# The last attention groups of a second block: softmax moved a round ahead, copies of probabilities first, one projection in halves

## The chip, the cores and the metric

The kernel runs on one core of a Trainium2 chip as a single launch. The metric is the device time of that launch in microseconds (us). A core has five engines that run their own instruction streams in order: TensorE (PE in the rows; PEld is its weight load), VectorE (DVE), ScalarE (ACT), GpSimd (POOL) and SyncE (SP), which here only issues loads. They meet through semaphores: an instruction waits until a counter that another engine raises has reached a value.

## The reference, cut to what matters

The program runs two blocks one after the other, each two layers deep, on 256 tokens of width 1024 in fp32. The first block (attention, then a mixture in which each token gathers 128 expert rows) takes most of the time and isn't touched. The second block's layer has four kinds of attention side by side, then an output projection and a wide feed-forward part:

```python
for l in range(DEPTH):                                   # 2 layers
    h = rms_norm_2(x, norm1_g[l])
    proj = h @ w_in[l]
    (a_cq, a_ckv, a_kr, b_q, b_k, b_v, c_q, c_k, c_v, d_q, d_k, d_v) = jnp.split(proj, splits, axis=-1)
    y_a = mla_mixer(a_cq, a_ckv, a_kr, ...)              # 4 heads, keys and values from a latent
    y_b = diff_mixer(b_q, b_k, b_v, ...)                 # 4 heads, difference of two softmaxes, then a norm per head
    y_c = swa_mixer(c_q, c_k, c_v, swa_sinks[l], ...)    # 4 heads, window of 128, a sink in the softmax
    y_d = na_mixer(d_q, d_k, d_v, na_rpb[l])             # 4 heads, a table of biases
    mix = jnp.concatenate([rms_norm_2(y_a, out_g_mla[l]), y_b,
                           rms_norm_2(y_c, out_g_swa[l]), rms_norm_2(y_d, out_g_na[l])], axis=-1)
    x = x + mix @ w_out[l]
    h = rms_norm_2(x, norm2_g[l])
    x = x + jnp.square(jax.nn.relu(h @ w_up[l])) @ w_down[l]
return rms_norm_2(x, final_norm_g)
```

## The kernel before, in words

Every engine has its own function (`pe_program`, `act_program`, `dve_program`, `sp_program`, `pool_program`), written out by hand in the order in which that engine shall run; nothing reorders it later. What one engine needs of another is a `wait_ge(*at(name, ...))`.

The attention of a layer of the second block is cut into ten groups, in the order `ORDER = ("d0", "d1", "d2", "d3", "m0", "m1", "w0", "w1", "n0", "n1")`: d are the difference heads, m the latent ones, w the window, n the table of biases; the digit of m, w and n is the half of the tokens. A group passes through these steps:

- scores on TensorE (`scores`) into one of two pairs of banks of the accumulator PS, used in turn;
- bias and row maximum on VectorE (`bias_and_max`). For w and n the bias is added into a buffer in BIG first, which frees the pair of banks; for d and m the maximum is read from PS;
- exponentials with row sums on ScalarE (`softmax`);
- sums turned into reciprocals on VectorE (`row_sums`), for d also the difference of the two softmaxes;
- transposes of the probabilities on TensorE (`p_transposes`) into the four single banks of PS, copied back to BIG by `evac_pT`: the even bank by ScalarE, the odd one by VectorE;
- the product with the values on TensorE (`values`), into a single bank again, and its scaled copy into H by VectorE (`attended`).

All engines run a loop of twelve rounds r. In round r TensorE makes the scores of group r, the values of group r-3 and the transposes of group r-2, and between them some other product: the projections C0, C1, D0, D1, D2 of the normed tokens (`project`), the lift of the latents (`lift`, rounds 0), and towards the end the transposes of finished sections (`mixed_T`) and the output projection (`out2`). Two groups' transposes are in flight at a time, so the single banks rotate: each use waits until the copy of the use four places before it is done (`singles.take`).

VectorE and ScalarE of the kernel before make, in round r, bias, maximum and exponentials of group r-1, then the row sums and the copies of group r-2:

```python
if 1 <= r <= 10:                       # act_program
    softmax(groups[r - 1], in_2)
...
if r > 1 and r != 10:
    evac_pT(groups[r - 2], in_2)
```

VectorE also squares the finished d heads (`tensor_tensor` into RT and a reduction) at the end of round 7, for a norm that ScalarE and VectorE finish in round 9. Round 6 holds D1, the product that all of this runs beside; round 9 holds the two halves of D2.

Ahead of the rounds TensorE projects the normed tokens. The tokens come in two halves of 128; for each half there is a transposition, whose copy into HT ScalarE and VectorE make, and then the latent projection (`project_A`), B0 and B1 (queries and keys of d). After B0 and B1 of both halves VectorE rotates them (`rope`, into RB, G in the rows), TensorE transposes the latents (`latent_T`) and makes B2, the values of d, and then transposes the rotated queries and keys (`slabs_T("dT", ...)`), which round 0 needs for its scores.

SyncE loads the weights into a ring of twelve places in BIG, in a fixed order. A place is free when the product that used it before is done, so a load waits for a counter of TensorE, and later loads wait behind it.

Of the kernel before, what the change touches and what calls it, by code (L numbers as in the profile page):

```python
# [188 lines left out]
def build(nc, I, out):  # L189
    with ExitStack() as ctx:  # L190
# [87 lines left out]
        Y = H  # L278
# [300 lines left out]
        def pe_program(e):  # L579
# [287 lines left out]
            def project(l, name, parts=(0, 1)):  # L867
                for t in parts if name in FIRST[l] else range(2):
                    have_hT(2 + l, t, 0)
                w = have(in_2, ("w2", l, name)).rearrange("p (k n) -> p k n", k=8)  # L870
                if name in FIRST[l]:
                    bk = singles.where[("prj", l, name)] = FIRST[l][name]
                    if l > 0:
                        pe.wait_ge(*at("v.xf", l - 1, 0))
                elif 0 in parts:
                    bk, freed = singles.take(("prj", l, name), (EVAC[name] + ".prj", l, name))
                    if freed:
                        pe.wait_ge(*at(*freed))
                bk = singles.where[("prj", l, name)]
                for z in parts:  # L880
                    zs = slice(z * 128, (z + 1) * 128)
                    for k in range(8):
                        if name in ("D0", "D1"):
                            p = mm(PS[:, bk, z * 256:(z + 1) * 256], w[:, k, zs], HT[:, k, :], k == 0, k == 7)
                        else:
                            p = mm(PS[:, bk, z * 256:(z + 1) * 256], HT[:, k, zs], w[:, k, :], k == 0, k == 7)
                if 1 in parts:
                    p.then_inc(*up("pe.prj", l, name))
# [97 lines left out]
            for l in range(L):  # L986
# [4 lines left out]
                transposes(2 + l, 1, 0, ("v.n1", l, 1))  # L991
                project_A(l, 1)
# [4 lines left out]
                project(l, "B2")  # L997
                slabs_T("dT", l, 0, 4)
                slabs_T("dT", l, 1, 4)
                groups = second_groups(l)  # L1000
                for r in range(12):
# [11 lines left out]
                    if r == 0:  # L1013
                        lift(l, 0)
# [53 lines left out]
        def act_program(e):  # L1068
# [287 lines left out]
            for l in range(L):  # L1356
# [25 lines left out]
                for r in range(12):  # L1382
# [5 lines left out]
                    if r == 10:  # L1388
                        mixed(l, "a")
                        evac_pT(groups[8], in_2)  # L1390
                    if 1 <= r <= 10:
                        softmax(groups[r - 1], in_2)
# [11 lines left out]
                    elif r == 4:  # L1404
                        slabs("wT", WT, l, 0, 3)
                        projected(l, "D0")
                    elif r == 9:
                        projected(l, "D2")
                    if r > 1 and r != 10:
# [28 lines left out]
        def dve_program(e):  # L1438
# [466 lines left out]

            def wide_sums(l, q):
# [74 lines left out]
            for l in range(L):  # L1981
# [30 lines left out]
                for r in range(12):  # L2012
                    if 1 <= r <= 10:
                        g = groups[r - 1]
                        bias_and_max(g, in_2, window_bias if g.key[2][0] == "w" else near_bias)
                    if r == 10:
                        mixed(l, "b")
                    if r > 1:
# [34 lines left out]
                    if r > 2:  # L2053
                        if r < 5:
                            v.wait_ge(*at("pe.hT", 2 + l, groups[r - 3].t, 0, 1))
                        attended(groups[r - 3])
                    if r == 9:
                        scaled(l, "a")
                        q = inverse("yb", 8, ("yb", l)).rearrange("p (t i) -> p t i", t=2)
# [6 lines left out]
                    if r == 7:  # L2066
                        yb = Y[:, :, 256:512].rearrange("p t (i d) -> p t i d", i=4)
                        jb = RT[:, 0:512].rearrange("p (t i d) -> p t i d", t=2, i=4)
                        tt(jb, yb, yb, ALU.mult).then_inc(*up("v.c"))
                        own()  # L2070
                        v.e.reduce_sum(sc("yb", 8), RT[:, 0:512].rearrange("p (i d) -> p i d", i=8), AX).then_inc(*up("v.subs", l))
# [206 lines left out]
```

## Time and profile before

| what | value |
|---|---|
| median of 3 runs (lowest to highest) | 2261.86 us (2261.33 to 2262.29) |
| the profiled execution's own time | 2260.58 us |
| its span, first to last instruction | 2258.8 us |
| TensorE, VectorE, ScalarE, GpSimd busy | 2033.3, 1477.3, 815.2, 613.5 us |
| mean granted clock of TensorE | 0.976 of full speed |
| second block, first layer's attention | some 1555 to 1684 us from the span's start |
| second block, second layer's attention | some 1901 to 2036 us |

The span and the profiled time are of one execution; the median is 1.28 us above that execution. In the timeline rows a line is a run of equal instructions: start, length, engine, source line, operation, what it writes and reads, count, and in brackets the idle time of that engine just before and what ended it. Instructions of TensorE overlap a little, so a run's length is some 0.1 to 0.2 us more than the distance to the next one's start. A matrix product in fp32 leaves two rows per instruction of the program.

### The profile page before, as it was taken

The page shows a single profiled execution, that of the slowest core. Times are in us where ns is not written, and L with a number is a line of the kernel's source. Part 1 is how long each engine was busy: PE and PEld are TensorE (multiplying, and loading weights), DVE is VectorE, ACT ScalarE, POOL GpSimd, SP SyncE. Part 2 cuts the span into 40 slices and gives each one's busy share as a digit, 9 for nine tenths or more (in the row PEclk, how much of TensorE's full clock was granted, in tenths as well). Part 3 has the DMA queues.
Part 4 walks back from the last instruction along what each step waited for, and adds up shares of the span by engine and source line. Part 5 has one row for each costly group of instructions (what it writes and reads, how often), then busy time and mean ns, then how long its engine had stood idle before and what let it go on. Part 6 is the DMA issues. An engine that isn't in the chain of part 4 may idle for free.

```text
span 2258.8 us, 25790 instructions
## 1 busy us (share of the span) xinstructions
PE 2033.3 (90%) x8812; PEld 1224.8 (54%) x8812; DVE 1477.3 (65%) x3289; ACT 815.2 (36%) x2373; POOL 613.5 (27%) x564
## 2 busy tenths in 40 slices
PE   6988998897979887999987888888999999999998
PEld 5555554453535433655443334335769945777953
DVE  2338867988557677787778657664457754546765
ACT  2215644545354344455444434443330001341000
POOL 1124435443444444444543444340000000000000
PEclk9999999998999999999999999999999999999999
DMA  9999999999999999999999999997332452242441
GB/s 391 418 425 427 404 427 426 427 426 421 427 426 421 426 427 404 426 401 427 427 427 426 422 427 426 427 427 292 114 148 112 158 202 111 94 187 93 154 182 65
DMA packets 106023, 750.91 MB, mean 332 GB/s; under 512 B 12034, under 2 KB 12322, under 8 KB 16035
## 3 DMA queue, kind: packets, MB, share of 16 engines
q0 software_dynamic: 80640, 587.24, 61.9%
q1 hardware_dynamic: 25252, 162.03, 18.3%
q8 instruction: 70, 1.15, 0.2%
q14 instruction: 61, 0.50, 0.1%
HBM read 748.17 MB, written 1.05 MB: 332 GB/s over the span
## 4 chain that ended last, share of the span: by engine, by line
PE 56%; DMA 20%; DVE 15%; ACT 6%; issue 2%; POOL 0%; DVEq 0%; SPq 0%; ACTq 0%; POOLq 0%
PE PS L583 54%; DMA BIG<-in_uv,EID 18%; DVE BIG L1796 6%; DMA MOD<-in_uv,EID 2%; ACT DG L1072 1%; ACT L1285 1%; DVE BIG L1450 1%; ACT L1276 1%; DVE H L1450 1%; PE PS L662 1%; ACT AV L1072 1%; ACT BIG L1148 1%; DVE BIG L1446 1%; DVE BIG L1460 1%; PE PS L695 0%
## 5 line engine op out<-in xcount | busy, mean ns | idle before, releaser
L583 PE MATMUL PS<-BIG,DG 128*128 128x512 f32 (+1 forms) x2156 | 901.0, 588 | 152.1 <-ACT DG L1072 127.9
L1796 DVE CUSTOM_DVE_ANT_0 BIG<-BIG,H 128x1024 f32<-128x1024 f32 x455 | 558.3, 1227 | 296.9 <-DMA BIG<-in_uv,EID 267.1
L523 POOL DMA_INDIRECT BIG<-in_uv,EID x455 | 523.1, 1150 | 724.7 <-PE PS L583 689.4
L583 PEld LDWEIGHTS PS<-BIG,DG 128*128 128x128 f32 (+1 forms) x2156 | 342.5, 182 | 609.1 <-issue 303.2
L1285 ACT ACTIVATE AV<-AV 128x1 f32<-128x1 f32 x512 | 103.1, 201 | 594.8 <-DVE AV L1796 590.6
L583 PE MATMUL PS<-BIG,HT 128*128 128x256 f32 (+3 forms) x1216 | 295.1, 399 | 3.4 <-ACT HT L1072 1.7
L583 PEld LDWEIGHTS PS<-BIG,HT 128*128 128x128 f32 x1216 | 226.6, 192 | 67.2 <-issue 39.4
L583 PEld LDWEIGHTS PS<-HT,BIG 128*128 128x128 f32 x1664 | 207.3, 192 | 35.7 <-issue 29.9
L1072 ACT ACTIVATE DG<-CST,AV 128x128 f32<-128x128 f32 x512 | 205.8, 402 | 49.0 <-PE PS L583 1.7
L583 PE MATMUL PS<-HT,BIG 128*128 128x128 f32 (+1 forms) x1664 | 213.8, 284 | 4.8 <-DMA BIG<-in_wq 4.8
L583 PE MATMUL PS<-BIG 128*128 128x512 f32 (+6 forms) x504 | 164.4, 497 | 1.8 <-DVE BIG L1446 1.8
L1072 ACT ACTIVATE AV<-AV,GATE 128x1 f32<-128x1 f32 x512 | 151.1, 295 | 18.9 <-ACT AV L1285 0.4
L1072 ACT ACTIVATE BIG<-PS 128x256 f32<-128x256 f32 (+5 forms) x138 | 59.4, 441 | 262.0 <-PE PS L583 221.5
L583 PE MATMUL PS<-MOD,DG 128*128 128x512 f32 (+1 forms) x276 | 116.1, 588 | 20.7 <-ACT DG L1072 18.4
L583 PEld LDWEIGHTS PS<-BIG 128*128 128x128 f32 (+3 forms) x504 | 78.9, 188 | 77.5 <-issue 74.9
L1450 DVE TENSOR_TENSOR BIG<-BIG 128x256 f32<-128x256 f32 (+2 forms) x176 | 96.2, 547 | 6.0
L1796 DVE CUSTOM_DVE_ANT_0 BIG<-MOD,H 128x1024 f32<-128x1024 f32 x57 | 70.0, 1228 | 39.4 <-DMA MOD<-in_uv,EID 34.2
L1119 ACT ACTIVATE ACC<-X 128x1024 f32<-128x1024 f32 x9 | 9.5, 1058 | 237.4 <-DVE X L1450 237.4
L583 PE MATMUL PS<-MOD,BIG 128*128 128x64 f32 (+1 forms) x320 | 84.9, 414 | 6.5 <-ACT BIG L1072 4.1
L583 PEld LDWEIGHTS PS<-MOD,DG 128*128 128x128 f32 (+1 forms) x276 | 42.9, 181 | 80.1 <-issue 38.6
L523 POOL DMA_INDIRECT MOD<-in_uv,EID x57 | 64.4, 1130 | 76.4 <-PE PS L583 73.1
L1450 DVE TENSOR_TENSOR MOD<-BIG 128x512 f32<-128x512 f32 (+1 forms) x48 | 41.8, 870 | 61.5 <-PE PS L583 57.7
(202 smaller groups left out, 1843.5 us busy)
## 6 DMA issues: line engine op xcount, KB each, us to landing
BIG<-in_wada POOLq DMA_DIRECT2D x43, 1024.0 KB
BIG<-in_wup SPq DMA_DIRECT2D x32, 1024.0 KB, 5.2
BIG<-in_wdn SPq DMA_DIRECT2D x32, 1024.0 KB, 5.9
BIG<-in_win SPq DMA_DIRECT2D x31, 1024.0 KB, 5.8
BIG<-in_wout SPq DMA_DIRECT2D x24, 1024.0 KB, 5.1
BIG<-in_wq SPq DMA_DIRECT2D x23, 1024.0 KB
BIG<-in_uv,EID POOLq DMA_INDIRECT x455
MOD<-in_wada POOLq DMA_DIRECT2D x5, 1024.0 KB
```

The source lines that it names most:

```text
L523: pool.e.indirect_dma_start(out=slot(u), out_offset=None, in_=I[f"uv{l}"], in_offset=bass.IndirectOffsetOnAxis(ap=EID[:, t * 128 + j:t * 1 ...
L583: return pe.e.matmul(dst, a, b, start=start, stop=stop)
L662: p = pe.e.transpose(PS[:, bk, c * 128:(c + 1) * 128], H[:, t, (c4 * 4 + c) * 128:(c4 * 4 + c + 1) * 128], ident)
L1072: return a.e.activation(dst, src, ACT.Copy, scale=scale)
L1119: a.e.activation(junk[:, o:o + w], src, ACT.Square, accum_out=s[:, i:i + 1]).then_inc(*up("a.c"))
L1148: ins = a.e.activation(P[:, i, :], src[:, i, :], ACT.Exp, bias=ng[:, i:i + 1], scale=g.scale, accum_out=rs[:, i:i + 1])
L1276: a.e.activation(GATE[:, j:j + 16], V[:, 32:48], ACT.Exp, bias=V[:, 48:49], scale=1.0, accum_out=V[:, 49:50]).then_inc(*up("a.gate", l, t, h))
L1285: a.e.activation(AV[:, j:j + 1], AV[:, j:j + 1], ACT.Gelu).then_inc(*up("a.gelu", p, b - 1))
L1446: return v.e.tensor_copy(dst, src)
L1450: return v.e.tensor_tensor(dst, a, b, op)
L1460: return v.e.scalar_tensor_tensor(out=dst, in0=a, scalar=s, in1=b, op0=op0, op1=op1)
L1796: v.e.tensor_tensor_reduce(out=JD, in0=slot(u)[:, 0:1024], in1=H[:, t, :], scale=1.0, scalar=0.0, op0=ALU.mult, op1=ALU.add, accum_out=AV[ ...
```

## The change

Only the second block's attention is edited, in three engines; both layers run the same code. TensorE: B2 is projected half by half, the first half between the transposition of the second half of the tokens and that half's latent projection, the second half where the whole was; one place of the rotating banks is passed over; the lift of the first half of the latents goes ahead of round 0's scores. VectorE and ScalarE: up to round 5 as before; in round 6 two groups, m1 and w0, get maximum and exponentials; from round 7 on the group of the round itself; ScalarE copies transposed probabilities ahead of the exponentials, except in round 9. The squares of the d heads move from round 7 to round 6, and in round 10 `mixed` of section b goes behind `attended`. As the list of groups is written on VectorE, `groups[r:r + 1]` also holds for round 0.

```diff
             def project(l, name, parts=(0, 1)):
-                for t in parts if name in FIRST[l] else range(2):
+                for t in parts if name in FIRST[l] or name == "B2" else range(2):
...
                 transposes(2 + l, 1, 0, ("v.n1", l, 1))
+                project(l, "B2", (0,))
                 project_A(l, 1)
                 project(l, "B0", (1,))
                 project(l, "B1", (1,))
                 latent_T(l, 0)
                 latent_T(l, 1)
-                project(l, "B2")
+                project(l, "B2", (1,))
+                singles.n += 1
                 slabs_T("dT", l, 0, 4)
                 slabs_T("dT", l, 1, 4)
+                lift(l, 0)
...
                     if r == 0:
-                        lift(l, 0)
                         lift(l, 1)
...
                     if r == 10:                                    # ScalarE
                         mixed(l, "a")
-                        evac_pT(groups[8], in_2)
-                    if 1 <= r <= 10:
+                    if r > 6:
+                        if r != 9:
+                            evac_pT(groups[r - 2], in_2)
+                        if r < 10:
+                            softmax(groups[r], in_2)
+                    elif r > 0:
                         softmax(groups[r - 1], in_2)
...
+                    elif r == 6:
+                        softmax(groups[6], in_2)
                     elif r == 9:
+                        evac_pT(groups[7], in_2)
                         projected(l, "D2")
-                    if r > 1 and r != 10:
+                    if 1 < r < 7:
                         evac_pT(groups[r - 2], in_2)
...
+            def squared(l):
+                yb = Y[:, :, 256:512].rearrange("p t (i d) -> p t i d", i=4)
+                jb = RT[:, 0:512].rearrange("p (t i d) -> p t i d", t=2, i=4)
+                tt(jb, yb, yb, ALU.mult).then_inc(*up("v.c"))
+                own()
+                v.e.reduce_sum(sc("yb", 8), RT[:, 0:512].rearrange("p (i d) -> p i d", i=8), AX).then_inc(*up("v.subs", l))
...
                 for r in range(12):                                # VectorE
-                    if 1 <= r <= 10:
-                        g = groups[r - 1]
+                    for g in groups[r - 1:r] if 0 < r < 6 else groups[5:7] if r == 6 else groups[r:r + 1]:
                         bias_and_max(g, in_2, window_bias if g.key[2][0] == "w" else near_bias)
-                    if r == 10:
-                        mixed(l, "b")
-                    if r > 1:
+                        if r == 6 and g is groups[5]:
+                            row_sums(groups[4], in_2)
+                            attended(groups[3])
+                            squared(l)
+                    if r > 1 and r != 6:
                         row_sums(groups[r - 2], in_2)
...
-                    if r > 2:
+                    if r > 2 and r != 6:
...
                         attended(groups[r - 3])
+                    if r == 10:
+                        mixed(l, "b")
...
-                    if r == 7:
-                        ...
-                        v.e.reduce_sum(sc("yb", 8), RT[:, 0:512].rearrange("p (i d) -> p i d", i=8), AX).then_inc(*up("v.subs", l))
```

On VectorE, from round 6 to the first copy of round 7, the kernel before has (PS is the accumulator, BIG holds probabilities and weights, H the attention's output, SC small statistics, MOD scratch):

```order
L1542 TENSOR_REDUCE SC<-PS 128x4
L1455 TENSOR_SCALAR SC<-SC 128x4
L1560 RECIPROCAL SC<-SC 128x4
L1446 COPY BIG<-PS 128x512
L1446 COPY H<-PS 128x128
L1446 COPY BIG<-PS 128x512
L1460 SCALAR_TENSOR_TENSOR BIG<-PS,CST 128x1024
L1542 TENSOR_REDUCE SC<-BIG 128x4
L1450 TENSOR_TENSOR SC<-SC,PARB 128x4
L1455 TENSOR_SCALAR SC<-SC 128x4
L1450 TENSOR_TENSOR SC<-PARB,SC 128x4
```

The first `COPY BIG<-PS` is that of D1, the second that of m0's transposed probabilities, and the rows from `SCALAR_TENSOR_TENSOR` on are bias and maximum of w0. In the changed kernel the same place reads (source lines are shifted, L1455 is the copy here):

```order
L1551 TENSOR_REDUCE SC<-PS 128x4
L1464 TENSOR_SCALAR SC<-SC 128x4
L1569 RECIPROCAL SC<-SC 128x4
L1455 COPY H<-PS 128x128
L1459 TENSOR_TENSOR MOD<-H 128x512
L1920 TENSOR_REDUCE SC<-MOD 128x8
L1469 SCALAR_TENSOR_TENSOR BIG<-PS,CST 128x1024
L1551 TENSOR_REDUCE SC<-BIG 128x4
L1459 TENSOR_TENSOR SC<-SC,PARB 128x4
L1464 TENSOR_SCALAR SC<-SC 128x4
L1459 TENSOR_TENSOR SC<-PARB,SC 128x4
L1455 COPY BIG<-PS 128x512 x2
```

The d heads' last output, their squares and all of w0's bias and maximum now stand ahead of the copy of D1, and the two copies follow each other.

On ScalarE, rounds 6 to 8 of the kernel before (L1148 the exponentials, four to a group, from PS for m1 and from BIG for w and n; L1152 those of the sinks; L1072 copies of transposed probabilities; L1119 the squares of round 9):

```order
L1148 ACTIVATE BIG,SC<-PS,SC 128x256 x4
L1072 ACTIVATE BIG<-PS 128x512
L1148 ACTIVATE BIG,SC<-BIG,SC 128x256 x4
L1152 ACTIVATE SC<-SC 128x4
L1072 ACTIVATE BIG<-PS 128x512
L1148 ACTIVATE BIG,SC<-BIG,SC 128x256 x4
L1152 ACTIVATE SC<-SC 128x4
L1072 ACTIVATE BIG<-PS 128x512
L1119 ACTIVATE ACC,SC<-H 128x256 x2
```

That is m1, the copy of m0, w0, the copy of m1, w1, the copy of w0, and the squares. In the changed kernel:

```order
L1150 ACTIVATE BIG,SC<-PS,SC 128x256 x4
L1150 ACTIVATE BIG,SC<-BIG,SC 128x256 x4
L1154 ACTIVATE SC<-SC 128x4
L1074 ACTIVATE BIG<-PS 128x512 x2
L1150 ACTIVATE BIG,SC<-BIG,SC 128x256 x4
L1154 ACTIVATE SC<-SC 128x4
L1074 ACTIVATE BIG<-PS 128x512
L1150 ACTIVATE BIG,SC<-BIG,SC 128x256 x4
L1121 ACTIVATE ACC,SC<-H 128x256 x2
```

The exponentials of w0, w1 and n0 have each gone up by one round, and stand behind the copy that was behind them: the order is now m1, w0, the copies of m0 and m1, w1, the copy of w0, n0, and the squares.

On TensorE, ahead of round 0, the difference between the two, at the second half of the tokens (L662 their transposition, 192 and 160 wide the latent projection):

```order
 L583 MATMUL PS<-BIG,HT 128x256 x16
 L662 MATMUL PS<-CST,H 128x128 x8
+L583 MATMUL PS<-BIG,HT 128x256 x8
 L583 MATMUL PS<-BIG,HT 128x192 x8
 L583 MATMUL PS<-BIG,HT 128x160 x8
```

and behind the latents' transposes (L896), where L916 are the transposes of the rotated queries and keys, 384 and 512 wide the lift, and 256 wide from BIG alone the scores of round 0:

```order
 L895 MATMUL PS<-CST,MOD 128x128
 L896 MATMUL PS<-CST,MOD 64x128
-L583 MATMUL PS<-BIG,HT 128x256 x16
+L583 MATMUL PS<-BIG,HT 128x256 x8
 L916 MATMUL PS<-CST,G 128x128 x8
-L583 MATMUL PS<-BIG 128x256 x4
 L583 MATMUL PS<-BIG 128x384 x2
 L583 MATMUL PS<-BIG 128x512
+L583 MATMUL PS<-BIG 128x256 x4
```

Eight of B2's sixteen products moved up to the place right behind the transposition, and one lift changed places with the scores. From round 1 on TensorE's order is the same as before; so are those of SyncE and GpSimd.

## Rows read from the trace of the kernel before

**Rows 1.** The page: busy time, share of the span and instructions by engine.
```profile
PE 2033.3 (90%) x8812; PEld 1224.8 (54%) x8812; DVE 1477.3 (65%) x3289; ACT 815.2 (36%) x2373; POOL 613.5 (27%) x564
```

**Rows 2.** Windows, first layer: stretch, length, busy by engine, granted clock, DMA share, GB/s.
```profile
1587.00:1636.00 49.00, 48.88 (x258) 39.17 (x258) 25.06 (x63) 17.40 (x61) 0.00 (x0) 1.00 0.35 129
1636.00:1650.40 14.40, 10.49 (x85) 8.64 (x83) 12.57 (x23) 6.28 (x24) 0.00 (x0) 1.00 0.41 146
1650.50:1657.30 6.80, 6.80 (x25) 5.99 (x24) 4.56 (x13) 5.45 (x14) 0.00 (x0) 0.50 0.00 0
```

**Rows 3.** Timeline of TensorE, first layer, rounds 6 to 10.
```profile
1636.18 1.04 PE L695 MATMUL PS<-CST,BIG 128*128 128x128 f32 x8
1637.15 1.14 PE L583 MATMUL PS<-BIG 64*128 64x256 f32 x8
1638.48 1.97 PE L583 MATMUL PS<-PRJ,BIG 128*128 128x64 f32 x16 [0.19 <-DVE BIG L1446]
...
1644.09 2.00 PE L583 MATMUL PS<-PRJ,BIG 128*128 128x64 f32 x16 [1.70 <-ACT BIG L1072]
...
1650.07 3.33 PE L583 MATMUL PS<-MOD,BIG 128*128 128x64 f32 x16 [2.03 <-ACT BIG L1072]
1653.20 5.71 PE L583 MATMUL PS<-BIG,HT 128*128 128x256 f32 x16
...
1659.62 3.62 PE L583 MATMUL PS<-BIG,HT 128*128 128x256 f32 x16
1664.46 1.97 PE L583 MATMUL PS<-MOD,BIG 128*128 128x64 f32 x16 [1.22 <-issue]
...
1668.19 0.66 PE L695 MATMUL PS<-CST,BIG 128*128 128x128 f32 x4 [0.45 <-DVE H L1450]
```

**Rows 4.** Timeline of TensorE, second layer, rounds 8 and 9.
```profile
1995.78 2.00 PE L583 MATMUL PS<-PRJ,BIG 128*128 128x64 f32 x16 [1.69 <-ACT BIG L1072]
...
2001.76 3.43 PE L583 MATMUL PS<-MOD,BIG 128*128 128x64 f32 x16 [2.03 <-ACT BIG L1072]
```

**Rows 5.** Timeline of TensorE, first layer, from the second half's transposition to round 0.
```profile
1564.44 11.92 PE L583 MATMUL PS<-BIG,HT 128*128 128x192 f32 x64 [0.93 <-DVE HT L1450]
...
1576.85 7.07 PE L583 MATMUL PS<-BIG,HT 128*128 128x256 f32 x32
...
1585.67 7.49 PE L583 MATMUL PS<-BIG 32*128 32x256 f32 x28 [0.88 <-DVE BIG L1446]
```

**Rows 6.** Timeline of VectorE, first layer: rotation, a maximum, rounds 6 to 8.
```profile
1576.39 0.69 DVE L1446 COPY MOD<-PS 128x512 f32<-128x512 f32 x1 [4.90 <-PE PS L583]
...
1579.99 1.22 DVE L1450 TENSOR_TENSOR G<-G,MOD 128x1024 f32<-128x1024 f32 x1
...
1593.38 1.22 DVE L1542 TENSOR_REDUCE SC<-PS 128x4 f32<-128x1024 f32 x1
...
1636.45 0.69 DVE L1446 COPY BIG<-PS 128x512 f32<-128x512 f32 x1 [7.88 <-PE PS L583]
...
1638.47 1.23 DVE L1460 SCALAR_TENSOR_TENSOR BIG<-PS,CST 128x1024 f32<-128x1024 f32 x1
...
1642.20 0.69 DVE L1446 COPY BIG<-PS 128x512 f32<-128x512 f32 x1
...
1643.65 0.69 DVE L2071 TENSOR_REDUCE SC<-MOD 128x8 f32<-128x512 f32 x1
```

**Rows 7.** Timeline of ScalarE, first layer, rounds 7 to 9.
```profile
1641.39 0.51 ACT L1148 ACTIVATE BIG<-BIG,SC 128x256 f32<-128x256 f32 x1 [3.97 <-DVE SC L1455]
...
1643.47 0.57 ACT L1072 ACTIVATE BIG<-PS 128x512 f32<-128x512 f32 x1
...
1649.92 0.40 ACT L1119 ACTIVATE ACC<-H 128x256 f32<-128x256 f32 x1
...
1652.63 1.28 ACT L1148 ACT_TABLE_LOAD   x1
```

**Rows 8.** DMA issues from 1551 to 1551.6 us: count, size, us to landing.
```profile
BIG<-in_win SPq DMA_DIRECT2D x2, 1024.0 KB, 9.1
```

More of the change, by code:

```diff
@@ L2056, in dve_program @@
                         attended(groups[r - 3])
+                    if r == 10:
+                        mixed(l, "b")
                     if r == 9:
                         scaled(l, "a")
+                        yb = Y[:, :, 256:512].rearrange("p t (i d) -> p t i d", i=4)
                         q = inverse("yb", 8, ("yb", l)).rearrange("p (t i) -> p t i", t=2)
@@ L2065, in dve_program @@
                         evac_pT(groups[r - 2], in_2)
-                    if r == 7:
[L2067 to L2070, printed above, removed]
-                        v.e.reduce_sum(sc("yb", 8), RT[:, 0:512].rearrange("p (i d) -> p i d", i=8), AX).then_inc(*up("v.subs", l))
                 scaled(l, "c")
```

## The prediction, made before the changed kernel ran

> **What bounds the kernel now.** The page comes first: TensorE is busy for 90% of the span [rows 1], so what can be won is its idle time, and what it loses at a lower clock. The windows by stage show where the second block loses any: from 1587 to 1636 us, rounds 0 to 6 of the first layer, TensorE is busy 48.88 of 49.00 us at a granted clock of 1.00; in the next 14.40 us only 10.49, while VectorE is busy 12.57; and in the 6.80 us behind that TensorE is always busy but at a granted clock of 0.50, the lower of its two levels (1.2 of 2.4 GHz) [rows 2]. The timeline then names the waits: in the last rounds the values wait 0.19 (m0), 1.70 (m1), 2.03 (w0) and 1.22 us (w1), and a transposition of n0 waits 0.45 [rows 3]. The low clock begins right after the wait of 2.03. The second layer has the same pair, 1.69 and 2.03 [rows 4], so I work out one layer and double it. Two more waits lie ahead of round 0: 0.93 us for the copy of the second half's transposed tokens and 0.88 us for the copy of the rotated queries and keys [rows 5].
>
> Why do the values wait? The rows name ScalarE, whose exponentials stood ahead of the copy. VectorE's own copy, the odd bank, is about as late: from w0's bias at 1638.47 to the end of the copy of m1 at 1642.20 + 0.69 = 1642.89 it works without a pause for 4.42 us, and then squares the d heads until 1643.65 + 0.69 = 1644.34, another 1.45 [rows 6]. TensorE has less per round: 1.80 for the values (1.97 less the overlap), 0.97 for the transposes (1636.18 to 1637.15) and about 1.07 for the scores, together 3.84 [rows 3]. So VectorE is the bound in rounds 7 to 9, ScalarE close behind; earlier, beside D1, VectorE sat idle for 7.88 us [rows 6].
>
> **The change, part by part.**
>
> *Ahead of round 0.* Half of B2, 7.07/2, about 3.46 us with the overlap taken off, now covers the copy of the tokens: the 0.93 goes. The lift, about 2.6 us by the mixed row of 7.49, covers the copy of queries and keys: the 0.88 goes. What is late next is the rotation. VectorE takes from 1576.39 to 1579.99 + 1.22 = 1581.21, so 4.86 us from the end of B1 [rows 6]. Before, TensorE had the latents' transposes and all of B2 for that time: until 1576.85 + 7.07 less the overlap, about 1583.76, so 2.55 to spare [rows 5]. With 3.46 of it gone a wait of 0.91, with the latency of a semaphore 0.95, arises; behind it queue the transposes, the lift and the scores. Net 0.93 + 0.88 - 0.95 = 0.86 us won per layer. The first half of B2 needs its weights earlier: they are the third of the loads, issued before 1551.6, and landed 9.1 us later [rows 8], so by 1560.7, ahead of 1563.5, where the transposition ends. No load is issued in another order, so no queue of SyncE or GpSimd changes; those behind a counter of TensorE move with it.
>
> *The second maximum of d0.* The new list gives round 0 a maximum that round 1 repeats: 1.22 us [rows 6] and a scaling, some 1.4 us, on VectorE ahead of the lifted queries' copies. These free a bank for C0, but TensorE has the second lift and round 1's scores before it, 2.6 + 1.07, about 3.7 us; the transposes of the m heads wait for VectorE only after C0. So I take 0. The bounds are 0 and its own 1.4 per layer, and since it adds work nothing below 0.
>
> *Round 6.* w0's bias, maximum and scalings take 2.92 us up to the first exponential (1638.47 to 1641.39) [rows 6, 7], the squares 1.45, both into VectorE's idle 7.88 beside D1. m1's maximum and d3's copy come first; I get w0's statistics by 1634.0. ScalarE then has w0's exponentials and sink, 2.08 us (1641.39 to the copy at 1643.47) [rows 7], done by 1636.1, and the copy of m0 could not start before 1636.8 anyway, as TensorE transposes at 1636.18 [rows 3]. So all of it is hidden, with 0.7 us to spare; without the cover it costs what it overruns.
>
> *Rounds 7 to 9.* In the times of before: D1's copy runs 1636.45 to 1637.14, m0's odd copy follows to 1637.94, and m0's values start at 1638.24 instead of 1638.48. VectorE starts w1 at 1638.35 and needs its 4.42 until 1642.77; ScalarE's copy of m1, now ahead of the exponentials, is done at 1641.2. m1's values start at 1642.85 instead of 1644.09: a wait of 0.75 us stays. VectorE goes on to n0 at once, as the squares are gone: the same 4.4 to 1647.3 (n has no sink to compare, but a sum for w0's), so w0's values start at 1647.3 instead of 1650.07 with a wait of 0.6: 2.77 us won so far. Between them lie 4.45 us of VectorE against 3.84 of TensorE, which is those 0.6 again.
>
> *The clock.* With waits of 0.75 and 0.6 in place of 1.70 and 2.03 I take the clock to stay at 1.00, as it did in the first layer through 0.19 and 1.70 [rows 2, 3]. Then w0's values take 1.97 instead of 3.33 and D2's first half 3.62 instead of 5.71, like its second half [rows 3]: 1.36 + 2.09 = 3.45, so 6.2.
>
> *From the second half of D2 on.* The 1.22 went because ScalarE copied D2 ahead of w1's probabilities. Now n1's exponentials and then w1's copy come first. Squares to exponentials took 1649.92 to 1652.63 + 1.28 = 1653.91, 4.0 us [rows 7]; from the end of n0's exponentials at 1647.8 that gives 1651.8, with 2.0 of exponentials and 0.57 of copy 1654.4, and TensorE ends D2 at 1657.0. The 1.22 goes, with 2.5 to spare. The 0.45, a bank that VectorE's `attended` frees, goes because `mixed` now stands behind it; `out2` needs that later. Sum 6.2 + 1.22 + 0.45 = 7.9 us per layer. What follows waits for weights whose loads hang on D2's end, which moves by some 6 of those 7.9; they land long before they are used.
>
> *Sum.* 0.86 + 7.9 = 8.8 per layer, 17.5 in two. The profiled execution took 2260.58 us (span 2258.8), so 2243.1; the median is 1.28 higher, so 2244.4 us. Its own range: all new waits gone as well would be 0.95 + 0.75 + 0.6 = 2.3 per layer, 2239.8; the second maximum at its full price 2247.2.
>
> **Rivals.**
>
> *The clock still falls.* Rounds 7 to 9 keep a wait in every round, and what runs between is short transposes and products 64 wide. If it falls as before, 3.45 per layer come back: 8.8 - 3.45 = 5.35, so 2251.2. Against it: the granted clock was 1.00 in all 14.40 us with two of the waits [rows 2]. The Trainium skill speaks for this rival: its page "TensorE: Matmul & The Clock Gate" tells in the section "A second HAM failure mode: psum-queue depth-cycling" of a kernel whose short idle times between groups of products made the clock swing. By that rule the time would be this rival's; the trace agrees only that waits precede the fall.
>
> *ScalarE takes over.* w0's exponentials now stand ahead of m0's copy, and n1's, behind a table load, ahead of w1's. If the second of these is late by more than its 2.5 us to spare, or the first by more than 0.7, TensorE waits for it: at most one set of exponentials with its copy, 2.08 + 0.57 = 2.65 per layer, so 2249.7. For it: ScalarE has been named as releaser at 1.70 and 2.03. Against it: it was idle for 3.97 us ahead of w0's exponentials [rows 7].
>
> *The change wins only at the entry.* If VectorE's chain starts in the last rounds where it did, because something in round 6 (a place in the ring, the scores) holds w0's bias until D1 is copied, the last rounds stay as they are: 2 x 0.86, so 2260.1, no change. Against it: w0's scores precede D1 on TensorE, and its place was freed by the lift.
>
> *Slower.* The clock falls at the first of the evenly spaced waits, near 1642, and, with a wait in each round, doesn't rise until `out2`. From there to 1660.8 TensorE has some 17.4 us of work at full clock; at half clock 17.4 more, against 8.8 won: 8.6 lost per layer, 2279. It decides once more than half of that stretch runs at 0.50. Against it: before, 0.50 held for 6.80 us and ended while the work was still short products.
>
> **Chances.** The forecast 0.76, the clock 0.11, ScalarE 0.05, entry only 0.05, slower 0.03. The range runs from 2239.8 to 2251.5, which takes in the first two rivals and leaves out some 0.1 with what may be missed below. What a measurement can tell from no change is 0.2%, 4.5 us: faster 0.91 (the first three, less a little), same 0.05, slower 0.04.
>
> **What the profile after would show.** The forecast is right step by step if in rounds 8 and 9 the values wait some 0.75 and 0.6 us, released by VectorE's copy and not by ScalarE; if the granted clock is 1.00 from round 7 to `out2`; if w0's values take about 1.97 and both halves of D2 about 3.6; if no wait stands ahead of w1's values and n0's transposes; and if a wait of about 0.95, released by the rotation on VectorE, stands ahead of the transposes in front of round 0, with none at the two old places. A clock of 0.50 there is the first rival, exponentials that end a wait the second, unchanged waits the third. The forecast is wrong if the two layers together win less than 13 us.

## The result and the profile after

| | before | after |
|---|---|---|
| median of six runs (range), us | 2261.6 (2257.27 to 2263.29) | 2243.74 (2242.82 to 2245.8) |
| profiled execution, us (its span) | 2260.58 (2258.8) | 2245.80 (2243.7) |
| second block in the trace, us | 703.27 | 685.01 |

The ratio is 0.9931, with a 95% interval of 0.9921 to 0.994. The medians lie 17.86 us apart, where 17.5 were forecast; the ratio makes it 15.6 us (13.6 to 17.9), so the forecast lies in the upper part of that interval. A page's span mixes in the first block, which the change doesn't touch and which took 3.15 us longer in the profiled execution of after. So I measure the second block alone, from the first product of B0 on TensorE to the end of the span. In before that product stands at 1555.51 (timeline of TensorE in before):

```profile
1555.51 7.08 PE L583 MATMUL PS<-BIG,HT 128*128 128x256 f32 x32
```

and in after 3.15 us later:

```profile
1558.66 7.07 PE L583 MATMUL PS<-BIG,HT 128*128 128x256 f32 x32
```

The block lost 18.26 us in the trace; the working gave 17.5.

The first lines to read are the page's busy times and the windows by stage, as for before [rows 1, 2]. Busy by engine in after:

```profile
PE 2029.8 (90%) x8812; PEld 1222.9 (55%) x8812; DVE 1480.0 (66%) x3293; ACT 814.8 (36%) x2373; POOL 605.2 (27%) x564
```

Windows of after: stretch, length, busy time of each engine, granted clock, DMA share, GB/s. The first three are rounds 0 to 6, 7 to 9 and 9 to 10 of the first layer, the last is rounds 8 to 10 and what follows in the second:

```profile
1589.00:1638.00 49.00, 48.88 (x262) 39.41 (x262) 31.03 (x73) 19.05 (x68) 0.00 (x0) 1.00 0.35 129
1638.00:1651.30 13.30, 11.90 (x98) 10.13 (x97) 11.32 (x19) 7.71 (x28) 0.00 (x0) 1.00 0.44 160
1651.30:1662.70 11.40, 11.40 (x76) 10.52 (x75) 5.80 (x16) 6.39 (x16) 0.00 (x0) 1.00 0.20 63
1990.00:2015.00 25.00, 24.34 (x143) 19.06 (x142) 11.86 (x30) 13.86 (x37) 0.00 (x0) 1.00 0.47 191
```

The share of busy time says nothing: 90% both times. The windows do: rounds 0 to 6 are as full as they were although VectorE does 6 us more in them, the rounds behind have 1.40 us of idle time instead of 3.91, and the clock is 1.00 where 6.80 us stood at 0.50 [rows 2].

TensorE's timeline of after, first layer, from round 6 to round 10, answers to [rows 3]:

```profile
1638.25 1.04 PE L695 MATMUL PS<-CST,BIG 128*128 128x128 f32 x8
...
1640.29 2.00 PE L583 MATMUL PS<-PRJ,BIG 128*128 128x64 f32 x16
...
1644.98 1.97 PE L583 MATMUL PS<-PRJ,BIG 128*128 128x64 f32 x16 [0.74 <-DVE BIG L1455]
...
1649.56 1.97 PE L583 MATMUL PS<-MOD,BIG 128*128 128x64 f32 x16 [0.66 <-DVE BIG L1455]
1651.37 3.67 PE L583 MATMUL PS<-BIG,HT 128*128 128x256 f32 x16
...
1655.75 3.62 PE L583 MATMUL PS<-BIG,HT 128*128 128x256 f32 x16
1659.20 1.89 PE L583 MATMUL PS<-MOD,BIG 128*128 128x64 f32 x16
...
1661.82 1.04 PE L695 MATMUL PS<-CST,BIG 128*128 128x128 f32 x8
1662.69 3.60 PE L583 MATMUL PS<-BIG,HT 128*128 128x512 f32 x8
```

The values of m0, m1, w0 and w1 start without a wait, after 0.74, after 0.66, and without one. Both waits left name VectorE's copy (L1455). The second layer has the same, and a wait for the rotation (L1459) ahead of round 0:

```profile
1929.30 1.09 PE L916 MATMUL PS<-CST,G 128*128 128x128 f32 x8 [0.80 <-DVE G L1459]
...
1987.57 1.97 PE L583 MATMUL PS<-PRJ,BIG 128*128 128x64 f32 x16 [0.74 <-DVE BIG L1455]
...
1992.15 1.97 PE L583 MATMUL PS<-MOD,BIG 128*128 128x64 f32 x16 [0.66 <-DVE BIG L1455]
```

Ahead of round 0 in the first layer of after, to be held against [rows 5], the two old waits are gone and the new one stands there:

```profile
1566.49 15.30 PE L583 MATMUL PS<-BIG,HT 128*128 128x256 f32 x80
...
1586.71 1.09 PE L916 MATMUL PS<-CST,G 128*128 128x128 f32 x8 [0.81 <-DVE G L1459]
1587.64 7.58 PE L583 MATMUL PS<-BIG 128*128 128x384 f32 x28
```

VectorE in after, against [rows 6]: w0's bias is now at 1633.43, ahead of D1's copy at 1638.45, and w1's bias to the end of m1's copy is 1640.41 to 1644.14 + 0.69 = 1644.83, the 4.42 us forecast. From m1's copy to w0's, the last row, it is 4.58 us: the next bias starts 0.14 behind the copy's end.

```profile
1633.43 1.23 DVE L1469 SCALAR_TENSOR_TENSOR BIG<-PS,CST 128x1024 f32<-128x1024 f32 x1
...
1638.45 0.69 DVE L1455 COPY BIG<-PS 128x512 f32<-128x512 f32 x1 [1.94 <-PE PS L583]
...
1640.41 1.22 DVE L1469 SCALAR_TENSOR_TENSOR BIG<-PS,CST 128x1024 f32<-128x1024 f32 x1 [0.40 <-PE PS L583]
...
1644.14 0.69 DVE L1455 COPY BIG<-PS 128x512 f32<-128x512 f32 x1
1644.97 1.23 DVE L1469 SCALAR_TENSOR_TENSOR BIG<-PS,BIG 128x1024 f32<-128x1024 f32 x1
...
1648.72 0.69 DVE L1455 COPY BIG<-PS 128x512 f32<-128x512 f32 x1
```

ScalarE in after, against [rows 7]: the sink's exponential of w0 (L1154), the copy of m0, which waits for TensorE for 0.37 us, and w1's copy, over at 1656.45, 2.75 us ahead of w1's values:

```profile
1638.33 0.19 ACT L1154 ACTIVATE SC<-SC 128x4 f32<-128x4 f32 x1
1638.89 0.60 ACT L1074 ACTIVATE BIG<-PS 128x512 f32<-128x512 f32 x1 [0.37 <-PE PS L695]
...
1655.88 0.57 ACT L1074 ACTIVATE BIG<-PS 128x512 f32<-128x512 f32 x1
```

### The profile page after: what moved, and what is told of

Same layout as the page of the kernel before. It is cut to its first block, busy times and chain, and to the rows that moved or that the text cites. A ratio compares the mean times of both kernels' runs of the same rounds, so it can differ in the third digit from the quotient of the medians.

```text
span 2243.7 us, 25793 instructions
## 1 busy us (share of the span) xinstructions
PE 2029.8 (90%) x8812; PEld 1222.9 (55%) x8812; DVE 1480.0 (66%) x3293; ACT 814.8 (36%) x2373; POOL 605.2 (27%) x564
## 3 DMA queue, kind: packets, MB, share of 16 engines
q8 instruction: 70, 1.15, 0.2%
## 4 chain that ended last, share of the span: by engine, by line
PE 54%; DMA 23%; DVE 14%; ACT 6%; issue 2%; POOL 0%; DVEq 0%; ACTq 0%; POOLq 0%
PE PS L583 53%; DMA BIG<-in_uv,EID 19%; DVE BIG L1805 6%; DMA MOD<-in_uv,EID 2%; DMA BIG<-in_wada 2%; ACT DG L1074 1%; ACT L1287 1%; DVE BIG L1459 1%; ACT L1278 1%; ACT AV L1074 1%; PE PS L695 1%; DVE H L1459 1%; DVE BIG L1469 1%; PE PS L662 0%; DVE SC L1551 0%
## 5 line engine op out<-in xcount | busy, mean ns | idle before, releaser
L523 POOL DMA_INDIRECT BIG<-in_uv,EID x455 | 515.2, 1132 | 733.2 <-PE PS L583 704.5
L583 PE MATMUL PS<-MOD,DG 128*128 128x512 f32 (+1 forms) x276 | 116.3, 579 | 17.5 <-ACT DG L1074 15.5
L1459 DVE TENSOR_TENSOR BIG<-BIG 128x256 f32<-128x256 f32 (+2 forms) x176 | 96.2, 547 | 6.0
L1459 DVE TENSOR_TENSOR MOD<-BIG 128x512 f32<-128x512 f32 (+1 forms) x48 | 41.8, 870 | 61.5 <-PE PS L583 57.7
## 6 DMA issues: line engine op xcount, KB each, us to landing
MOD<-in_wada POOLq DMA_DIRECT2D x5, 1024.0 KB, 15.6
```

The lines of the kernel that those rows point to most:

```text
L523: pool.e.indirect_dma_start(out=slot(u), out_offset=None, in_=I[f"uv{l}"], in_offset=bass.IndirectOffsetOnAxis(ap=EID[:, t * 128 + j:t * 1 ...
L583: return pe.e.matmul(dst, a, b, start=start, stop=stop)
L1459: return v.e.tensor_tensor(dst, a, b, op)
```

## The experiments

The theory: the gain is the sum of parts that don't touch each other, the entry, VectorE's statistics moved out of rounds 7 to 9, and the clock that stays up because the waits are short. The rival: ScalarE's order (copies first) is what counts, as the releasers of [rows 3] say, and the rest is ornament. The kernels ran in three groups, each beside runs of before on the same chip (medians of before there: 2260.4 for the first four below, 2258.46, and 2261.31 for the last two). "Block" is the second block in the profiled execution, 703.27 in before and 685.01 in after.

### The entry alone, and the rounds alone

Entry alone is before with these lines of the change (and the two halves of B2 allowed); rounds alone is after without them:

```diff
+                project(l, "B2", (0,))
                 project_A(l, 1)
...
-                project(l, "B2")
+                project(l, "B2", (1,))
+                singles.n += 1
...
+                lift(l, 0)
```

> The kernel before with the entry part alone: B2 by halves, the lift of the first half ahead of round 0's scores. Theory, the parts add up: some 0.9 us per layer, 1.8 in all, so about 2259.8 us; in the trace the waits of 0.93 and 0.88 are gone, one of about 0.8 for the rotation on VectorE stands in their place, and the waits of rounds 8 and 9 (1.70 and 2.03) and the stretch at a granted clock of 0.50 are as before. Rival, the earlier start also takes the edge off the later waits or the low clock: 5 us or more.

> The changed kernel with the entry put back: B2 whole, the lift behind the scores; the last rounds as changed. Theory, the parts add up: 7.9 us per layer, so about 2245.8 us, with waits of 0.74 and 0.66 in rounds 8 and 9, a granted clock of 1.00, and the entry's 0.93 and 0.88 back. Rival, the two parts need each other: less than 10 us won against the kernel before.

Entry alone: 2256.83 us, ratio 0.9982 (0.9973 to 0.9991), block 698.91. Rounds alone: 2244.53, ratio 0.993 (0.9917 to 0.9944), block 687.11. So the rounds carry nearly all, 16.2 of 18.26 in the trace, and the entry is worth 2.1 on top of them, near the 1.8 expected. Alone the entry won 4.4 in the trace and 4.1 by the ratio (2.0 to 6.1), more than that. TensorE's timeline of entry alone, second layer, rounds 8 and 9, shows why:

```profile
1994.85 3.17 PE L583 MATMUL PS<-PRJ,BIG 128*128 128x64 f32 x16 [1.69 <-ACT BIG L1074]
1997.81 1.91 PE L695 MATMUL PS<-CST,BIG 128*128 128x128 f32 x8
...
2001.67 2.27 PE L583 MATMUL PS<-MOD,BIG 128*128 128x64 f32 x16
2003.78 3.67 PE L583 MATMUL PS<-BIG,HT 128*128 128x256 f32 x16
```

Here the clock fell one group earlier, on m1's values (3.17 us, not 2.00). The half-speed work filled the time in which w0's values had waited 2.03 us [rows 4], and D2 ran at full clock. From m1's values to D2 it is 8.93 us; with the old waits at full clock it would be 7.78 (2001.76 - 1995.78 + 1.80, [rows 3, 4]). So the low clock cost 1.15 us here and not 3.4, since much of it ran beside a wait that was there anyway; its price depends on where it falls. In the first layer of this run it fell behind w0's wait, as in before; no run tells whether the earlier start or chance moved it in the second.

### Copies first alone, and the squares put back

Copies first is before with only ScalarE's order changed; the squares are put back in after:

```diff
+                    if r in (7, 8):                    # before: copies first
+                        evac_pT(groups[r - 2], in_2)
                     if 1 <= r <= 10:
                         softmax(groups[r - 1], in_2)
...
                     elif r == 9:
+                        evac_pT(groups[7], in_2)
                         projected(l, "D2")
-                    if r > 1 and r != 10:
+                    if r > 1 and r not in (7, 8, 9, 10):
                         evac_pT(groups[r - 2], in_2)
```

```diff
                             attended(groups[3])
-                            squared(l)
...
+                    if r == 7:                         # after: squares put back
+                        squared(l)
```

> The kernel before with ScalarE's order alone changed: in rounds 7 and 8 the copy of the transposed probabilities ahead of the exponentials, in round 9 that of w1 ahead of D2's copy. VectorE keeps its order and its work. Theory, VectorE is the bound and ScalarE only just behind it: m1's values wait for VectorE's odd copy, 0.5 us instead of 1.70, w0's values start only 0.7 us earlier, so their wait is some 2.4 us and the granted clock still falls to 0.50; the 1.22 ahead of w1's values goes. About 0.7 + 1.2 = 1.9 us per layer, so about 2257.8 us. Rival, ScalarE's order was the bound, as the rows name it: the waits and the low clock go, 1.70 + 2.03 + 3.45 + 1.22 = 8.4 us per layer, about 2244.8 us.

> The changed kernel with the squares of the d heads put back to the end of round 7 on VectorE (1.45 us). Theory, VectorE is the bound: m1's wait stays at 0.74, w0's grows from 0.66 to about 2.1 us, 2.9 us in two layers, about 2246.6 us if the granted clock stays at 1.00; if one wait of that size is enough to bring it down to 0.50, 3.45 per layer more, about 2253.5 us. I expect the clock to fall. Rival, ScalarE is the bound: no change, 2243.7 us.

Copies first: 2252.68 us, ratio 0.9972 (0.9961 to 0.9983), block 694.0. The rival gave 2244.8, some 15.6 us won; by the ratio it is 6.3 (3.8 to 8.8), so the rival falls. TensorE's timeline of copies first, first layer:

```profile
1643.55 1.97 PE L583 MATMUL PS<-PRJ,BIG 128*128 128x64 f32 x16 [0.64 <-DVE BIG L1449]
...
1649.95 1.97 PE L583 MATMUL PS<-MOD,BIG 128*128 128x64 f32 x16 [2.48 <-DVE BIG L1449]
1651.76 3.67 PE L583 MATMUL PS<-BIG,HT 128*128 128x256 f32 x16
```

As soon as ScalarE is early, VectorE is the releaser, and w0's wait of 2.03 becomes 2.48. The two waits together are 3.12 us instead of 3.73. What I hadn't expected is the clock: w0's values take 1.97 and D2 3.67 behind the longest wait that any of these kernels has there. In the second layer they take longer behind the same wait:

```profile
1996.17 2.68 PE L583 MATMUL PS<-MOD,BIG 128*128 128x64 f32 x16 [2.47 <-DVE BIG L1449]
```

The windows of copies first, around w0's values in the first and the second layer:

```profile
1645.00:1660.00 15.00, 12.52 (x82) 11.07 (x81) 13.30 (x26) 9.43 (x28) 0.00 (x0) 1.00 0.01 2
1991.00:2006.00 15.00, 12.53 (x73) 11.00 (x73) 11.75 (x25) 9.29 (x27) 0.00 (x0) 0.89 0.01 5
```

Same code, same waits (2.48 and 2.47): the first layer kept 1.00, the second had 3.41 us at 0.50 (a mean of 0.89 over 15.00 us). The expectation had the full low stretch in both layers; the clock accounts for most of the 5 us by which the run beats it (3.4 in the first layer, about half of that in the second).

With the squares put back: 2252.97 us, ratio 0.9964 (0.995 to 0.9978), block 692.91, 7.9 us worse than after; 2253.5 was expected, with the full low stretch in both layers. The wait for w0's values is 2.10 in both layers instead of 0.66, and the clock falls behind it:

```profile
1650.48 2.12 PE L583 MATMUL PS<-MOD,BIG 128*128 128x64 f32 x16 [2.10 <-DVE BIG L1455]
...
1996.18 3.00 PE L583 MATMUL PS<-MOD,BIG 128*128 128x64 f32 x16 [2.10 <-DVE BIG L1455]
```

It stays at 0.50 for 3.41 us in the first layer and for 6.83 in the second, which over 14.00 us makes the means of 0.88 and 0.76 in the rows below. Windows around w0's values with the squares put back, first and second layer:

```profile
1648.00:1662.00 14.00, 11.90 (x63) 10.23 (x59) 8.40 (x21) 8.60 (x25) 0.00 (x0) 0.88 0.01 1
1994.00:2008.00 14.00, 11.89 (x53) 10.45 (x52) 8.11 (x21) 8.60 (x25) 0.00 (x0) 0.76 0.00 0
```

The layers lose 3.11 and 4.79 us against after: 1.44 each by the wait, so 1.67 and 3.35 by the clock, half of each low stretch. 1.45 us of VectorE in the wrong round cost 3 to 5 us per layer in this trace.

What ScalarE's new order is worth inside the change was not measured: no run has VectorE's part of it with ScalarE's copies behind the exponentials.

### The waits filled: the clock by itself

This is before with useless products into the accumulator ahead of m1's and w0's values, which overwrite them. The waits stay, but TensorE works through them:

```diff
+FILL = dict(m1=(512, 256), w0=(512, 512))
...
+                for n in FILL.get(g.key[2], ()):
+                    mm(PS[:, bk, 0:n], ident, HT[:, 0:n // 256, :], True, True)
                 for z in range(g.banks):
```

> The kernel before with idle time alone taken away, not the waits: ahead of m1's values TensorE makes two products of no use (512 and 256 wide), ahead of w0's values two of 512, into the bank that the values then overwrite; they fit into the waits of 1.70 and 2.03. Theory, the low clock comes of TensorE's idle time in these waits and has its own price: the granted clock stays at 1.00, w0's values take 1.97 and D2's first half 3.62, nothing else moves, 3.45 us per layer, 6.9 in all, so about 2253.5 us. Rival, the low clock comes of the kind of work around it (short transposes, products 64 wide) or costs nothing: no change, 2260.4 us.

TensorE's timeline with the waits filled, first layer (the two rows from HT and CST are the added products):

```profile
1644.22 1.56 PE L584 MATMUL PS<-HT,CST 128*128 128x512 f32 x4
1645.98 2.00 PE L584 MATMUL PS<-PRJ,BIG 128*128 128x64 f32 x16 [0.20 <-ACT BIG L1075]
...
1649.86 1.98 PE L584 MATMUL PS<-HT,CST 128*128 128x512 f32 x4
1651.96 2.00 PE L584 MATMUL PS<-MOD,BIG 128*128 128x64 f32 x16
1653.79 3.67 PE L584 MATMUL PS<-BIG,HT 128*128 128x256 f32 x16
```

w0's values start 94.55 us behind B0, as in before (94.56), so nothing is won up to there; the values take 2.00 and D2 3.67: the clock stays up, and the block is 696.59, 6.68 shorter, 3.34 per layer where the term was 3.45. So in the trace the term is shown by itself. The timed runs give less: 2255.79 us, ratio 0.9985 (0.9976 to 0.9995), some 3.4 us (1.1 to 5.4). The profiled execution of before has the long low stretch in both layers, and shorter ones in its other executions would explain the difference, but that isn't shown: the mean granted clock of before's 15 runs in this group is 0.9764 against 0.9794 for the 11 with the waits filled, nearly as far apart as in the two profiled executions (0.976 and 0.979). Before's runs in this group were also its fastest, a median of 2258.46. Why the timed runs give less than the trace isn't settled.

### The second maximum, and the odd bank moved to ScalarE

One maximum is after with another list of groups; in the second edit, on top of it, ScalarE also makes VectorE's copy of m1 and w0, the one that both remaining waits name:

```diff
-                    for g in groups[r - 1:r] if 0 < r < 6 else groups[5:7] if r == 6 else groups[r:r + 1]:
+                    for g in groups[max(r - 1, 0):r] if r < 6 else groups[5:7] if r == 6 else groups[r:r + 1]:
```

```diff
+def copier(g, z):
+    return "a" if g.key[2] in ("m1", "w0") else engine_of(z)
...
-                for z in range(1, g.banks, 2):
+                for z in [z for z in range(g.banks) if copier(g, z) == "v"]:
```

> The changed kernel without the second maximum of d0 in round 0. Theory, it was hidden: no change, 2243.7 us, and no wait of TensorE in rounds 0 to 2 in either kernel. Rival, it delays a bank that C0 needs: up to 1.4 us per layer, 2241 us.

> The changed kernel (with one maximum of d0) where ScalarE also copies the odd banks of m1's and w0's transposed probabilities, 0.7 us of VectorE's round each. Theory, VectorE's 4.45 us per round against TensorE's 3.84 is the bound: with 3.7 the waits of 0.74 and 0.66 go, 1.4 us per layer, 2.8 in all, so about 2240.9 us. Rival, ScalarE then becomes the bound, with 2.65 and 0.5 more per round: its exponentials end late and waits on ScalarE stand there, no change or slower, 2243.7 us or more.

One maximum: 2243.81 us, ratio 0.9935 (0.9921 to 0.9948), block 685.02 against 685.01: the second maximum cost nothing. With ScalarE's copies: 2240.53 us, ratio 0.9918 (0.9905 to 0.9932), block 682.03, 3.0 shorter where 2.8 were expected. TensorE's timeline of it, first layer, without a wait:

```profile
1642.20 2.00 PE L587 MATMUL PS<-PRJ,BIG 128*128 128x64 f32 x16
...
1646.08 2.00 PE L587 MATMUL PS<-MOD,BIG 128*128 128x64 f32 x16
```

and VectorE's, where n0's bias now waits for TensorE's scores:

```profile
1642.33 1.22 DVE L1473 SCALAR_TENSOR_TENSOR BIG<-PS,BIG 128x1024 f32<-128x1024 f32 x1 [0.26 <-PE PS L587]
```

The values stand 3.88 us apart, TensorE's own 3.84 and little more. This shows what held them 4.58 apart in after: VectorE's round, which there was 4.58 from copy to copy.

### The rotation's wait, and two lifts together

Both lifts go ahead of the scores, the first also ahead of the transposes that wait for the rotation (on top of the last edit; VectorE takes the first lift ahead of its next slab copy):

```diff
                 singles.n += 1
+                lift(l, 0)
                 slabs_T("dT", l, 0, 4)
                 slabs_T("dT", l, 1, 4)
-                lift(l, 0)
+                lift(l, 1)
...
-                    if r == 0:
-                        lift(l, 1)
```

> The kernel with ScalarE's copies and, at the entry, the lift of the first half ahead of the transposes of the rotated queries and keys and that of the second half behind them; VectorE makes the first lifted queries ahead of its copy. Theory, the lift of 2.6 us covers the rotation's wait of 0.81, the second lift the copy behind the transposes: 0.8 us per layer beyond ScalarE's copies, 1.6 in all, so about 2239.3 us. Rival, VectorE's lifted queries come late and hold the second lift's bank or the scores, so that the wait only moves: 2240.9 us or more.

The result was 2236.81 us, ratio 0.9905 (0.989 to 0.992), block 677.51: 4.52 shorter than without this edit, where 1.6 was the wait to be won. The wait is gone. For the other 2.9 the only other difference I found was that the scores of d0 and d1 now follow each other, with no lift between them. To tell the two apart, one kernel has the lifts together but the transposes first, and the other is the same as the last:

```diff
                 slabs_T("dT", l, 1, 4)
                 lift(l, 0)
+                lift(l, 1)
```

> The kernel with ScalarE's copies, and both lifts ahead of the scores of d0, so that the scores of d0 and d1 follow each other; the rotation's wait of 0.81 stays. Theory, from the trace of the kernel with both edits: the scores of d0 use rows 0 to 63 of the array and those of d1 rows 64 to 127, a quarter of the rows each product, and all eight side by side take 1.1 us instead of twice 1.07; so 1.2 us per layer, 2.5 in all, go against the 2240.5 us of the kernel with ScalarE's copies, about 2238.0 us, and the second block is 2.5 us shorter in the trace. Rival, the 1.4 us per layer that the kernel with both edits won beyond the wait of 0.81 came of the lift's place: no change against 2240.5 us.

> The kernel with ScalarE's copies and the lifts around the transposes once more, beside the kernel with paired scores on the same chip. Theory: it has the paired scores too and hides the wait of 0.81, so it is 1.6 us faster than the paired scores alone, about 2236.4 us. Rival: no difference between the two.

Lifts together: 2238.04 us, ratio 0.99 (0.9882 to 0.9917), block 679.54, 2.49 shorter than with ScalarE's copies alone, as expected; the rotation's wait of 0.81 stays. The last kernel again: 2235.25 us, ratio 0.9892 (0.9875 to 0.9909), block 677.51. It takes the remaining 2.03 (1.6 by the wait, the rest because without a wait a group overlaps the one before it again). TensorE's timeline of lifts together, from the transposes on:

```profile
1585.24 1.09 PE L920 MATMUL PS<-CST,G 128*128 128x128 f32 x8 [0.81 <-DVE G L1462]
1586.17 6.34 PE L587 MATMUL PS<-BIG 128*128 128x384 f32 x28
```

The same 28 rows (two lifts and the scores of d0 and d1, two rows to a product) took 7.58 in after and take 6.34. Grouped by line and form, the 16 rows of score products with ScalarE's copies alone (busy us, mean ns of one, idle us before):

```profile
L587 PE MATMUL PS<-BIG 32*128 32x256 f32 x16 | 2.3, 400 | 0.0
```

and in the last kernel:

```profile
L587 PE MATMUL PS<-BIG 32*128 32x256 f32 x16 | 1.2, 400 | 0.0
```

One product still takes 400 ns, but TensorE is busy with them for half as long: they run side by side. This version beats both kernels: in its group it is 26 us faster than before's 2261.31 by the medians, 24 by the ratio.

## Why the prediction was right, step by step

First layer, positions counted from the start of B0, so that the first block drops out:

| step, up to | before | after | won | forecast |
|---|---|---|---|---|
| entry: transposes of m0 (1636.18, 1638.25) | 80.67 | 79.59 | 1.08 | 0.86 |
| rounds 7 to 9: values of w0 | 94.56 | 90.90 | 2.58 | 2.77 |
| clock: second half of D2 | 104.11 | 97.09 | 3.36 | 3.45 |
| w1's copy: values of w1 | 108.95 | 100.54 | 1.39 | 1.22 |
| up to the product behind n0's transposes | 113.18 | 104.03 | 0.74 | 0.45 |

The sum is 9.15 for 8.8; the rest of the block's 18.26, 9.11, is won in the second layer. The last position in before, which [rows 3] don't have, is

```profile
1668.69 3.60 PE L583 MATMUL PS<-BIG,HT 128*128 128x512 f32 x8
```

*The bound.* That VectorE was nearly as late as the ScalarE named in [rows 3], and would hold the rounds at 4.45 us, is shown twice: copies first swaps the releaser and takes only 0.6 of the two waits, and ScalarE's copies bring 3.88. In after the values stand 1649.56 - 1644.98 = 4.58 apart, the wait of 0.66 for 0.6: VectorE's round is 4.58 too, and the sum had left out the 0.14 between the end of a copy and the next bias. That is most of the 0.19 by which rounds 7 to 9 fell short.

*The entry.* The new wait for the rotation is 0.81, not 0.95, which accounts for 0.14 of the 0.22 gained over the forecast. The second maximum is free, as taken.

*Round 6.* It is hidden, but with 0.37 us to spare where I had 0.7: w0's exponentials and sink ended at 1638.52, in the times of before (2.07 earlier) at 1636.45, where I had 1636.1. Of the terms, this one was the nearest to failing.

*The clock.* Right in after, and shown by itself with the waits filled, at 3.34 per layer in the trace. But the working rests on the low stretches of one execution. In the timed runs filling the waits is worth some 3.4 us (1.1 to 5.4), not 6.9. So the sum of 17.5 is 0.8 short of what the profiled block won, and close to the medians of the first group, but the ratio there gives 15.6; and against the before of the second group (2258.46) the change with one maximum wins about 14.7 (1 - 0.9935). That the median fell within 0.7 us of the forecast is in part luck.

*The small waits.* The two that went at w1's values and n0's transposes brought 0.17 and 0.29 more than their length: behind a wait a group doesn't overlap the one before it. D2's second half takes 3.62, and w1's values start 3.45 behind its start where nothing waits (1655.75 to 1659.20). That accounts for the 0.17; the 0.29 I take to be the same.

*The rivals.* The clock falling again would have shown 0.50; it was 1.00 in all four windows. Behind that rival stood the Trainium skill, "TensorE: Matmul & The Clock Gate", section "A second HAM failure mode: psum-queue depth-cycling", which tells of short idle times between groups of products that make the clock swing. A fall behind such a wait is seen here with waits of 2.10 (squares put back) but not with 0.74 and 0.66, nor in one layer with 2.48. ScalarE as the next bound did not come about (2.75 us to spare at w1's copy), nor did an unchanged end, nor the slower case. One argument against the slower case was misread: in before the 0.50 ended at 1657.30, during D2's first half with its products 256 wide [rows 2, 3], not among the short products.

## What to carry to other kernels

The engine named as releaser is the last one, not the only late one: before moving its work, follow the other producers of the same wait and see how far behind they are, since the wait can only shrink to theirs. Work that is needed much later (here the squares, 1.45 us) should leave the round in which its engine is the bound, and go where that engine sits idle. A term that rests on a clock that falls behind waits should be sized from several executions; a filler in the wait measures it by itself in a trace, and the timed runs say whether it holds there.

## What the hardware showed that I had not expected

- Whether the clock falls behind a wait, and for how long, isn't set by that wait's length alone: 2.48 us left it at 1.00 and 2.47 in the next layer brought 3.41 us of 0.50 (copies first); 2.10 brought 3.41 and 6.83 (squares put back). Half of the low stretch is lost where TensorE is busy, and less where a wait would have stood (entry alone, 1.15 us for 6.83).
- Score products of 32 rows of two groups that lie on different rows of the array take 1.2 us for their 16 rows of the profile when they follow each other in the program, and 2.3 when a lift stands between them. The Trainium skill states in "TensorE: Matmul & The Clock Gate", section "Part 3: Packing small matmuls — row/col tiling", that small products on distinct groups of 32 rows run at the same time; the trace agrees, and shows that it is won or lost by the order of the program: d0's scores use two such groups, d1's the other two.
